# Two norm hand-overs of a two-block transformer kernel: VectorE over pairs of feature tiles, the per-feature factors on ScalarE

## The reference, cut to what matters

```python
merged = jax.nn.sigmoid(ga) * y_attn + jax.nn.sigmoid(gb) * y_conv
h = h + rms_norm(merged @ w_out, mix_post_g)       # norm 1
u = rms_norm(h, ffn_pre_g)
gate, up = jnp.split(u @ w_gate_up, 2, axis=-1)
f = (jax.nn.silu(gate) * up) @ w_down
h = h + rms_norm(f, ffn_post_g)                    # norm 2
...                                                # second block:
h2 = h @ ev_w_in                                   # (even layer, then an RWKV-7 layer)
```

## Time and profile before

| | us |
|---|---|
| median of 3 runs (2559.2 to 2572.19) | 2566.4 |
| the profiled execution's own time | 2561.83 |
| its span, first to last instruction | 2560.0 |
| PE busy | 2463.7 (96%) |
| DVE busy | 1588.1 (62%) |
| ACT busy | 1161.6 (45%) |

### The profile page before, as it was taken

The page is one execution under the profiler, slowest core; times in us unless marked ns, Lnnn a source line. Parts: engine busy times, 40 slices in busy tenths (PEclk is TensorE's granted clock), DMA queues, the critical chain, the costliest instruction groups (busy, mean ns, idle before and its releaser), DMA issues.

```text
span 2560.0 us, 37908 instructions
## 1 busy us (share of the span) xinstructions
PE 2463.7 (96%) x15318; PEld 2116.4 (83%) x15318; DVE 1588.1 (62%) x2148; ACT 1161.6 (45%) x1541; POOL 72.3 (3%) x94
## 2 busy tenths in 40 slices
PE   8999999999899999999999899999899999999896
PEld 7888888888788888888888688888687888888675
DVE  6888887875656655655444656666622684356566
ACT  5444554654544444444444355654436201255544
POOL 0000000000000000000000000000000201012000
PEclk9999999999999999999999999999999999999998
DMA  6564455555365566556555455455633456322362
GB/s 232 186 195 159 155 173 189 177 184 185 99 192 187 187 192 189 174 189 198 189 189 189 133 176 175 160 172 190 198 115 107 147 166 206 130 93 81 113 222 91
DMA packets 419455, 427.68 MB, mean 167 GB/s; under 512 B 25344, under 2 KB 414464, under 8 KB 418320
## 3 DMA queue, kind: packets, MB, share of 16 engines
q1 hardware_dynamic: 414880, 403.07, 49.2%
q0 software_dynamic: 4400, 22.19, 2.6%
HBM read 415.19 MB, written 9.96 MB: 166 GB/s over the span
## 4 chain that ended last, share of the span: by engine, by line
PE 75%; DVE 14%; ACT 5%; DMA 3%; issue 2%; SPq 0%; ACTq 0%; DVEq 0%
PE GP L1826 69%; PE SB L1826 6%; DVE wL L1017 5%; ACT wH L502 3%; DMA raw<-w_gate_up_dram 2%; DVE y L1017 1%; DVE acc L1023 1%; DVE hf L1017 1%; DMA raw<-w_in_dram 1%; DVE x L1017 1%; DVE j L1017 1%; DVE f L1023 1%; DVE ga L1017 1%; SPq L481 0%; PE SB L1830 0%
## 5 line engine op out<-in xcount | busy, mean ns | idle before, releaser
L1017 DVE TENSOR_TENSOR wL<-raw,wH 128x1024 fp32r<-128x1024 f32 x664 | 804.5, 1226 | 548.5 <-ACT wH L502 546.7
L502 ACT CAST wH<-raw 128x1024 fp32r<-128x1024 f32 x664 | 682.7, 1046 | 540.4 <-PE GP L1826 247.3
L1826 PE MATMUL GP<-u2B,wH 128*128 128x512 f32 x1408 | 443.1, 396 | 0.0
L1826 PE MATMUL GP<-uB,wH 128*128 128x512 f32 x1152 | 363.5, 397 | 0.0
L1826 PEld LDWEIGHTS GP<-u2B,wL 128*128 128x128 f32 x1408 | 263.6, 188 | 78.3 <-DVE wL L1017 9.3
L1826 PE MATMUL GP<-u2B,wL 128*128 128x256 f32 x1408 | 280.2, 280 | 9.7 <-DVE u2B L1023 6.1
L1826 PEld LDWEIGHTS GP<-uB,wL 128*128 128x128 f32 x1152 | 216.8, 189 | 54.0 <-DVE wL L1017 3.1
L1826 PE MATMUL GP<-xB,wH 128*128 128x512 f32 x768 | 243.3, 398 | 0.0
L1826 PE MATMUL GP<-uB,wL 128*128 128x256 f32 x1152 | 232.7, 283 | 3.2 <-DVE wL L1017 2.3
L1826 PE MATMUL GP<-xk,dw 128*128 128x256 f32 x1024 | 229.5, 382 | 4.6 <-DVE xk L1023 4.6
L1826 PEld LDWEIGHTS GP<-xk,dw 128*128 128x128 f32 x1024 | 194.9, 191 | 33.4 <-issue 6.5
(11 more groups left out here) (408 smaller groups left out, 3025.2 us busy)
## 6 DMA issues: line engine op xcount, KB each, us to landing
raw<-w_gate_up_dram SPq DMA_DIRECT2D x352, 256.0 KB, 3.6
raw<-w_in_dram SPq DMA_DIRECT2D x288, 256.0 KB, 3.4
raw<-ev_w_in_dram SPq DMA_DIRECT2D x192, 256.0 KB, 3.4
raw<-w_down_dram SPq DMA_DIRECT2D x176, 256.0 KB, 3.4
raw<-w_out_dram SPq DMA_DIRECT2D x64, 256.0 KB, 3.6
raw<-ev_w_out_dram SPq DMA_DIRECT2D x64, 256.0 KB, 3.5
dw<-w_k_dram SPq DMA_DIRECT2D x64, 256.0 KB, 3.4
dw<-w_r_dram SPq DMA_DIRECT2D x64, 256.0 KB, 3.3
```

Source lines behind the costliest of these rows:

```text
L502: e.copy(wH[SLOT[i]], raw[m % RAW].rearrange("p (k n) -> p k n", k=4)).then_inc(s["hi"], 1)
L1017: return e.tensor_tensor(o, a, b, op)
L1826: return e.matmul(o, l, r, start=start, stop=stop, skip_group_check=True)
```

## The change

For both norms the 16 tiles become 9 groups: tile 0, tile 1, and then seven pairs. Four things differ:

1. `empty_post` on ScalarE multiplies the slab by the norm's factors g right behind its squares: two more ACTIVATE of 128 x 256 for each of the 8 slabs of `w_out` and of `w_down`. VectorE then needs only the token factor rsA.
2. `post_group` on VectorE: f times rsA and x plus f are tensor_tensors of 128 x 512 for a pair.
3. Behind norm 1 ScalarE writes x times g_fpre into f1 in float32 (one ACTIVATE per tile), then casts it to u2H (one cast per group, behind a wait on its own semaphore `th`); VectorE's low part is the plain difference of the two. Behind norm 2 only the width changes.
4. `group_range` gives step 0 the groups 0 to 3 (tiles 0 to 5), then each step one group; VectorE's low parts lag one group.

```diff
+GROUPS = [range(0, 1), range(1, 2)] + [range(i, i + 2) for i in range(2, DT, 2)]
+FED = 16 + 2 * len(GROUPS)
...
+        def group_range(u):
+            return range(min(u + 3, len(GROUPS) + 1) if u else 0, min(u + 4, len(GROUPS) + 1))
...                                    # ScalarE, empty_post
                     e.activation(to, o, ACT.Square).then_inc(s[key + "_sq"], 1)
+                    e.wait_ge(s[key + "_sq"], 3 * j + 1)
+                    for i in (2 * j, 2 * j + 1):
+                        e.activation(fb[:, i, :], fb[:, i, :], ACT.Copy, scale=V(gname, i)).then_inc(s[key + "_sq"], 1)
...                                    # ScalarE, u2_group
-                    e.wait_ge(s["h1"], i + 1)
-                    e.activation(u2H[:, i, :], x[:, i, :], ACT.Copy, scale=V("g_fpre", i)).then_inc(s["th"], 1)
+                    e.wait_ge(s["h1"], g.stop)
+                    for i in g:
+                        ins = e.activation(f1[:, i, :], x[:, i, :], ACT.Copy, scale=V("g_fpre", i))
+                    ins.then_inc(s["th"], 1)
+                    e.wait_ge(s["th"], 16 + 2 * k + 1)
+                    e.copy(u2H[:, span(g), :], f1[:, span(g), :]).then_inc(s["th"], 1)
...                                    # ScalarE, x_group
-                    e.wait_ge(s["h2"], i + 1)
-                    e.copy(xH[:, i, :], x[:, i, :]).then_inc(s["th"], 1)
+                    e.wait_ge(s["h2"], g.stop)
+                    e.copy(xH[:, span(g), :], x[:, span(g), :]).then_inc(s["th"], 1)
...                                    # VectorE
-            def post_tile(i, fb, gname, key, done):
-                stt(fb[:, i, :], fb[:, i, :], V(gname, i), rsA, ALU.mult, ALU.mult).then_inc(s[key + "_f"], 1)
-                e.wait_ge(s[key + "_f"], i + 1)
-                tt(x[:, i, :], x[:, i, :], fb[:, i, :], ALU.add).then_inc(s[done], 1)
+            def post_group(k, fb, key, done):
+                q = span(GROUPS[k])
+                n = len(GROUPS[k])
+                if k == 0:
+                    e.wait_ge(s[key + "_sq"], 24)
+                tt(fb[:, q, :], fb[:, q, :], rep(rsA, n), ALU.mult).then_inc(s[key + "_f"], 1)
+                e.wait_ge(s[key + "_f"], k + 1)
+                tt(x[:, q, :], x[:, q, :], fb[:, q, :], ALU.add).then_inc(s[done], n)
...
-                    stt(u2L[:, i - 1, :], x[:, i - 1, :], V("g_fpre", i - 1), u2H[:, i - 1, :].bitcast(F32),
-                        ALU.mult, ALU.subtract).then_inc(s["tl"], 1)
+                    tt(u2L[:, span(g), :], f1[:, span(g), :], u2H[:, span(g), :].bitcast(F32), ALU.subtract).then_inc(s["tl"], len(g))
...                                    # both engines (TensorE's wait on the last squares: 8 becomes 22)
-            stream("w_gate_up", empty_gu, lambda u: [u2_tile(i) for i in tile_range(u, 1)])
+            stream("w_gate_up", empty_gu, lambda u: [u2_group(k) for k in group_range(u) if k])
...
-            stream("ev_w_in", empty_ev, lambda u: [x_tile(i) for i in tile_range(u, 0)])
+            stream("ev_w_in", empty_ev, lambda u: [x_group(k) for k in group_range(u)])
```

More of the change, by code:

```diff
@@ L453, in two, with span @@
             return GP[PAIR[n]][:, :, h]
+        def group_range(u):
+            return range(min(u + 3, len(GROUPS) + 1) if u else 0, min(u + 4, len(GROUPS) + 1))
+        def span(g):
+            return slice(g.start, g.stop)
         def tile_range(u, first):
@@ L634, in empty_conv, with empty_post @@
                 e.copy(mH[:, 2 * j:2 * j + 2, :], ga[:, 2 * j:2 * j + 2, :]).then_inc(s["mh"], 1)
-            def empty_post(fb, sqb, total, key):
+            def empty_post(fb, sqb, total, key, gname):
                 def empty(n, sl, j):
@@ L651, in post_rt, with u2_group @@
                 e.activation(rsA, SB[0][:, 0:256], ACT.Sqrt, bias=C("eps")[:, 0:1], scale=1.0 / DM).then_inc(s[key + "_rt"], 1)
-            def u2_tile(i):
-                if i < DT:
-                    if i == 0:
+            def u2_group(k):
+                if k < len(GROUPS):
+                    g = GROUPS[k]
+                    if k == 0:
                         e.wait_ge(s["unit"], U1["w_out"])
-                    e.wait_ge(s["h1"], i + 1)
-                    e.activation(u2H[:, i, :], x[:, i, :], ACT.Copy, scale=V("g_fpre", i)).then_inc(s["th"], 1)
+                    e.wait_ge(s["h1"], g.stop)
[4 more added lines that the diff above has]
+                    e.copy(u2H[:, span(g), :], f1[:, span(g), :]).then_inc(s["th"], 1)
             def scale2():
@@ L699, in empty_gu, with x_group @@
                         high_gu(g)
-            def x_tile(i):
-                if i < DT:
-                    if i == 0:
+            def x_group(k):
+                if k < len(GROUPS):
+                    g = GROUPS[k]
+                    if k == 0:
                         e.wait_ge(s["unit"], U1["w_down"])
-                    e.wait_ge(s["h2"], i + 1)
-                    e.copy(xH[:, i, :], x[:, i, :]).then_inc(s["th"], 1)
+                    e.wait_ge(s["h2"], g.stop)
+                    e.copy(xH[:, span(g), :], x[:, span(g), :]).then_inc(s["th"], 1)
             def empty_ev(n, sl, j):
@@ L991, in scalar_program @@
             stream("w_conv_o", empty_conv)
-            stream("w_out", empty_post(f1, sq1, sum1, "p1"))
+            stream("w_out", empty_post(f1, sq1, sum1, "p1", "g_post"))
             post_rt("p1")
-            u2_tile(0)
-            stream("w_gate_up", empty_gu, lambda u: [u2_tile(i) for i in tile_range(u, 1)])
-            stream("w_down", empty_post(f2, sq3, sum3, "p2"))
+            u2_group(0)
+            stream("w_gate_up", empty_gu, lambda u: [u2_group(k) for k in group_range(u) if k])
+            stream("w_down", empty_post(f2, sq3, sum3, "p2", "g_fpost"))
             post_rt("p2")
-            stream("ev_w_in", empty_ev, lambda u: [x_tile(i) for i in tile_range(u, 0)])
+            stream("ev_w_in", empty_ev, lambda u: [x_group(k) for k in group_range(u)])
             stream("ev_w_out", empty_ln("l1", y1, wp[0]))
@@ L1212, in behind @@
                     if 0 < j < 7:
-                        e.wait_ge(s[key + "_sq"], j + 1)
+                        e.wait_ge(s[key + "_sq"], 3 * j + 1)
                         if j > 1:
@@ L1222, in post_rs, with u2_group @@
                 e.wait_ge(s[key + "_rs"], 1)
-            def post_tile(i, fb, gname, key, done):
-                stt(fb[:, i, :], fb[:, i, :], V(gname, i), rsA, ALU.mult, ALU.mult).then_inc(s[key + "_f"], 1)
-                e.wait_ge(s[key + "_f"], i + 1)
-                tt(x[:, i, :], x[:, i, :], fb[:, i, :], ALU.add).then_inc(s[done], 1)
[L1229 to L1233, removed]
-                    stt(u2L[:, i - 1, :], x[:, i - 1, :], V("g_fpre", i - 1), u2H[:, i - 1, :].bitcast(F32),
-                        ALU.mult, ALU.subtract).then_inc(s["tl"], 1)
+            def post_group(k, fb, key, done):
+                q = span(GROUPS[k])
+                n = len(GROUPS[k])
+                if k == 0:
+                    e.wait_ge(s[key + "_sq"], 24)
+                tt(fb[:, q, :], fb[:, q, :], rep(rsA, n), ALU.mult).then_inc(s[key + "_f"], 1)
+                e.wait_ge(s[key + "_f"], k + 1)
+                tt(x[:, q, :], x[:, q, :], fb[:, q, :], ALU.add).then_inc(s[done], n)
+            def u2_group(k):
+                if k < len(GROUPS):
+                    post_group(k, f1, "p1", "h1")
+                if k:
+                    g = GROUPS[k - 1]
+                    e.wait_ge(s["th"], 16 + 2 * k)
+                    tt(u2L[:, span(g), :], f1[:, span(g), :], u2H[:, span(g), :].bitcast(F32), ALU.subtract).then_inc(s["tl"], len(g))
             def scale2():
@@ L1264, in scaled_gu, with x_group @@
                     tt(hL[:, q, :], o, hH[:, q, :].bitcast(F32), ALU.subtract).then_inc(s["hl"], 1)
[L1266 to L1271, removed]
+            def x_group(k):
+                if k < len(GROUPS):
+                    post_group(k, f2, "p2", "h2")
+                if k:
+                    g = GROUPS[k - 1]
+                    e.wait_ge(s["th"], FED + k)
+                    tt(xL[:, span(g), :], x[:, span(g), :], xH[:, span(g), :].bitcast(F32), ALU.subtract).then_inc(s["tl"], len(g))
             def empty_ev(n, sl, j):
@@ L1981, in behind @@
                     if j == 7:
-                        e.wait_ge(s[key + "_sq"], 8)
+                        e.wait_ge(s[key + "_sq"], 22)
                         stat(SB[0][:, 0:256], [sqb[:, 2 + i, :] for i in range(2)], False, True).then_inc(s[key + "_st"], 1)
```

## The result

The changed kernel took 2585.66 us (median of 4, 2581.57 to 2587.88) against 2563.78 (2559.2 to 2572.19): a ratio of 1.007, interval 1.0052 to 1.0087. Timed again later on one chip with the experiments it was 2587.18 against 2567.88, 1.0072 (1.0056 to 1.0088). It is slower, by some 18 us (13 to 22 by the interval).

What follows compares the result with a forecast made beforehand. Bound: a ring of ScalarE and VectorE behind the norms, where TensorE (busy 96%) stands still. +6.6 and +6.8 make +13.4, +12 taken: median 2566.4 + 12 = 2578 us; own range 2573 to 2584, with rivals 2563 to 2588.

Steps and rivals of the forecast that it cites:

- The ring: Behind both norms, ScalarE and VectorE wait on each other in turns: 5.14 us behind norm 1, 4.19 behind norm 2.
- The shift of one step: Behind both norms, units 2, 4, 6 get their last two tiles' low parts a step late: +9.0 to +15.8 us.
- The waits in mid-unit: Behind the norms, TensorE standing still in the middle of even units: four waits of 2.7 to 3.8 us.
- Hand-over 1: Stretch from norm 1's reciprocal to ScalarE's first w_gate_up slab copy: +4.6 at full clock, +6.6 or +7.8 with half clock.
- C4: Start of ScalarE's cast of unit 4: at 649.8 us behind norm 1, 1421.3 behind norm 2.
- gated turns: Turns behind the norms whose next cast waits for TensorE to finish two tiles: 4.29 + 2.56 + 0.23 us at half clock.
- Hand-over 2: Stretch from norm 2's reciprocal to ScalarE's first ev_w_in slab copy: +4.4 at full clock, +6.8 or +8.0 with half clock.
- The sentence on the clock: The Trainium skill's warning would have all four mid-unit waits re-throttle TensorE, +13.4; rows leave room for some starting late.
- ScalarE's factors in the emptying: In w_out and w_down, two ACTIVATEs a slab, 16 us in all, covered by casts made ahead: cost 0.
- a rival at +8: In the emptying, half of the slabs pass ScalarE's delay on: +8 on top of 12, 2586 us, chance 0.07.
- The sum: Both hand-overs added: +9.0 at full clock, +13.4 half in gated units, +15.8 half at the ends too; +12 taken.
- half clock in the gated units: Behind both norms, TensorE at half rate after waiting in units whose end releases a cast: +6.6 + 6.8 = +13.4.

Runs made afterwards that it cites:

- e1: The changed kernel with each group taken one step earlier (step 0 takes tiles up to 7); ratio to the kernel before 1.0011 (1.0002 to 1.0021).
- e2: The kernel before, single tiles, with only the schedule moved late (step 0 takes tiles up to 4); ratio to the kernel before 1.0053 (1.0039 to 1.0067).
- e3: The kernel before with only the norm's factors moved to ScalarE in the emptying; ratio to the kernel before 0.9996 (0.9983 to 1.0009).
- e4: The changed kernel with six useless matmuls ahead of the third tile of units 2, 4 and 6 of both matrices; ratio to the kernel before 1.0042.
- e8: The changed kernel run again without edit, source of its second profile; 2587.18 us against 2567.88 for the kernel before, ratio 1.0072.
- e6: e1 with each slab's factors moved to just ahead of ScalarE's copy of the next slab; ratio to the kernel before 1.001 (0.9999 to 1.0022).

## Why the prediction was right, and where its sizes were off

It forecast slower by 12, 2578 us, range 2563 to 2588; measured were 2585.66. The interval of the ratio puts the rise at 13 to 22 us, so the 12 was somewhat too small. The mechanism was the right one, and by its steps:

*The ring, not VectorE's work, sets the hand-over.* Right. VectorE's instructions cost what was forecast (0.685 to 0.692), it was busy less, and the time rose. The turns: 5.14 forecast, 5.19 and 5.20 measured; behind norm 2 4.19, measured 4.26 and 4.27.

*The shift of one step.* Right, and shown by e1 and e2 from both sides. The waits in mid-unit and the casts released by TensorE are where they were forecast, but for the cast of unit 8 in hand-over 1 of the second profile. The Trainium skill's advice on operands of 512 elements or more ("VectorE: DVE Perf Modes", section on the TRN2 errata) held for the size of an instruction (0.69 us for 512 columns against 0.85 for two of 256) and not for the kernel: the hand-overs grew by 15.6 us, and with the schedule set right (e1) they were still 0.3 us longer than before.

*Hand-over 1: +6.6 forecast, +9.2 and +7.9 measured.* The term that was mis-sized is C4. I had unit 0's last two tiles at full clock (1.39) and C4 at 12.1 us behind the reciprocal; they ran at half rate, and C4 came at 13.91, 1.8 later (0.3 of it since TensorE's first tile came later). The gated turns were 7.38 and 7.28 against 7.1. In the second profile C4 came at 13.61.

*Hand-over 2: +6.8 forecast, +6.4 and +7.8 measured*, by two errors that cancelled in the first profile. C4 was late there too (13.96 behind the reciprocal against 12.6), while the gated turns took 6.12 and not 7.1: the waits of 2.53 and 2.52 us in mid-unit were not followed by the half rate this time. In the second profile they were, and the gated turns took 6.76 and 7.37. The sentence on the clock had allowed for both.

*ScalarE's factors in the emptying: cost 0.* Wrong, though small: w_out was 0.7 to 1.2 us longer in four profiles with the factors behind the squares and 2.2 in the fifth (e3), where 0.9 was half clock in the last sums; in w_down TensorE's wait for the sum was 0.2. I had compared ScalarE's 1.0 us with how far ahead units are cast, and had not followed what stands behind those casts: VectorE's sum of squares, for which TensorE waits at once. The prediction named this as a rival at +8; it was about an eighth of that.

*The clock.* An estimated 1.1 to 2.4 us in hand-over 1 and up to 1.4 in hand-over 2 (e4). The Trainium skill's warning ("TensorE: Matmul & The Clock Gate", section on HAM oscillation) that waits for operands re-throttle again and again held for four waits of 2.32 to 3.47 us in hand-over 1 of the two profiles; in hand-over 2 it held for waits of 2.53 and 2.52 us in the second profile and not in the first.

*The sum.* 15.6 in the hand-overs and 0.9 in w_out, 16.5, where 12 was taken and 13.4 was its value with half clock in the gated units. The chance of slower by over 0.5% was put at 0.38, which looks low: it followed from a centre just under that bound, and from leaving C4 at full clock.

*What stays open.* The profiled spans differ by 19.4 and 25.4. Of the second, 6.6 lie in w_gate_up and w_down, which took between 729.25 and 737.95 us in these nine profiles, with the same work but for the factors in w_down. In e8 TensorE waited 6.1 us there for wL, in the first profile of the changed kernel 1.8 and in the kernel before 3.4 (groups of TensorE in that stretch, e8_again first):

```profile
L1849 PE MATMUL GP<-u2B,wL 128*128 128x256 f32 x1352 | 269.1, 280 | 6.4 <-DVE wL L1035 6.1
```

```profile
L1849 PE MATMUL GP<-u2B,wL 128*128 128x256 f32 x1352 | 267.7, 279 | 2.1 <-DVE wL L1035 1.8
```

Whether the late schedule makes that more likely was not tried. Open too are the 2 us ahead of w_out and the total of e4.

## What to carry to other kernels

When a producer and a consumer pass work in steps, regrouping the producer's work changes which step the last piece comes in: check, piece by piece, that each is made no later than the step in which it is wanted, before counting what the wider instructions save. Where two engines hand work back and forth, count the turn of that ring and not the busier engine's load: here a cast of 0.62 us a turn on ScalarE, put there to spare VectorE, made the turn longer (4.85 us before, 5.20 changed), and taking it away again made it shorter (4.55). And an instruction put into a queue "with room" is to be followed through all that stands behind it, until something that another engine waits for.

## What the runs showed that I had not expected

TensorE fell to half rate after some waits of about 2.5 us in mid-unit and not after others: behind norm 2 of the kernel before it did, somewhat late, after 2.52 us; in the changed kernel waits of 2.53 and 2.52 at the same places were followed by it in the second profile and not in the first. At the third tile of unit 4 in hand-over 1, it set in at once behind a wait of 2.32 us and only 1 us late behind one of 3.39. So the length of the wait alone does not tell. The same instructions in hand-over 1 took 48.83 and 47.55 us in two executions, and 41.57 and 43.00 in e1 and e6, at clocks of 0.77, 0.83, 0.84 and 0.81: a difference of one or two us between single profiles of such a hand-over can be the clock's alone.
